# A hybrid attention step on one Trainium2 core: the stores of the attention rows issued by SP among its loads in place of ACT

## What is computed

```
for grp in range(B_GROUPS):
    q, k, v = qkv[:, :, 0, grp], qkv[:, :, 1, grp], qkv[:, :, 2, grp]
    o, lse = _dilated_attn_prompt(q, k, v, B_DILATIONS[grp], P['rel_bias_table'], grp)
    outs.append(o)
    lses.append(lse)
alpha = jax.nn.softmax(jnp.stack(lses, axis=0), axis=0)
attn = jnp.sum(alpha[..., None] * jnp.stack(outs, axis=0).astype(jnp.float32), axis=0)
```

## Time and profile before

| | |
|---|---|
| three runs | 2621.84, 2625.69 and 9907.76 us (one far outlier), median 2625.69 |
| profiled execution | 2629.4 us, span of its instructions 2627.7 us |
| PE busy | 2521.2 us, 96% of the span |
| DVE, ACT, POOL busy | 926.3, 581.7, 511.8 us |
| granted PE clock, mean | 0.981 of full speed |
| DMA, mean | 95 GB/s |

### The profile page before, as it was taken

How to read it: one execution, slowest core, us unless ns; L and a number is a source line. 1 busy time by engine, 2 the same in 40 slices (tenths; PEclk the granted TensorE clock), 3 DMA queues, 4 the chain that set the end, 5 groups by cost and what they waited for, 6 DMA issues and landing times.

```text
span 2627.7 us, 36573 instructions
## 1 busy us (share of the span) xinstructions
PE 2521.2 (96%) x16287; PEld 2398.7 (91%) x16287; DVE 926.3 (35%) x1684; ACT 581.7 (22%) x888; POOL 511.8 (19%) x209
## 2 busy tenths in 40 slices
PE   6999889889999999999999999999999999999998
PEld 5997777568999999999999899988999999999997
DVE  5267653457122222112224512446122222222225
ACT  3212223415211111111112411144211111111112
POOL 2211010102212211212212322122212222112220
PEclk7999999899999999999999999999999999999999
DMA  7522332771212222221221578311111111111101
GB/s 244 192 63 87 98 122 77 244 251 33 81 57 73 97 72 74 81 80 66 81 85 60 171 265 294 126 34 33 49 34 47 49 49 49 47 35 49 49 33 67
DMA packets 163819, 249.10 MB, mean 95 GB/s; under 512 B 6148, under 2 KB 150809, under 8 KB 162382
## 3 DMA queue, kind: packets, MB, share of 16 engines
q1 hardware_dynamic: 150618, 179.29, 20.8%
q0 software_dynamic: 4784, 63.31, 7.0%
q10 hardware_dynamic: 8260, 4.15, 0.6%
HBM read 228.04 MB, written 62.54 MB: 111 GB/s over the span
## 4 chain that ended last, share of the span: by engine, by line
PE 73%; DVE 3%; ACT 2%; DMA 1%; issue 1%; SPq 0%; DVEq 0%
PE ps L2223 66%; PE ps L2323 3%; PE ps L2450 1%; PE ps L2280 1%; DVE h_lo L1489 1%; DVE x L1424 1%; DMA w_raw<-in_e_w_out 0%; PE ps L2346 0%; ACT h_hi L1086 0%; PE ps L2643 0%; ACT nt L1088 0%; DVE nt L1463 0%; PE ps L2458 0%; ACT w_hi L1036 0%; ACT h_hi L1090 0%
## 5 line engine op out<-in xcount | busy, mean ns | idle before, releaser
L2043 POOL TENSOR_TENSOR w_lo<-w_raw,w_hi 128x2048 fp32r<-128x2048 f32 x93 | 432.4, 4649 | 1745.0 <-ACT w_hi L1036 1744.8
L2223 PE MATMUL ps<-h_hi,w_hi 128*128 128x352 f32 x2976 | 656.8, 329 | 6.1 <-ACT tmp L1041 3.0
L2223 PE MATMUL ps<-h_hi,w_lo 128*128 128x352 f32 x2976 | 642.3, 323 | 0.0
L2223 PE MATMUL ps<-h_lo,w_hi 128*128 128x352 f32 x2976 | 641.6, 324 | 0.0
L2223 PEld LDWEIGHTS ps<-h_hi,w_hi 128*128 128x128 f32 x2976 | 502.4, 189 | 26.0 <-issue 23.1
L2223 PEld LDWEIGHTS ps<-h_hi,w_lo 128*128 128x128 f32 x2976 | 511.3, 188 | 0.0
L2223 PEld LDWEIGHTS ps<-h_lo,w_hi 128*128 128x128 f32 x2976 | 506.7, 188 | 0.0
L1516 DVE SCALAR_TENSOR_TENSOR x<-ps,mod,x 128x704 f32<-128x704 f32 (+1 forms) x384 | 270.6, 746 | 285.4 <-PE ps L2223 285.4
L1565 DVE TENSOR_TENSOR tmp<-ps,tmp 128x1056 f32<-128x1056 f32 x44 | 55.3, 1258 | 722.8 <-PE ps L2223 722.8
L1036 ACT ACTIVATE w_hi<-w_raw 128x2048 fp32r<-128x2048 f32 x92 | 175.8, 1911 | 505.4 <-PE ps L2223 389.6
L2223 PE MATMUL ps<-mid_hi,w_hi 128*128 128x352 f32 x1104 | 241.2, 327 | 0.7 <-issue 0.6
(11 more groups left out here) (328 smaller groups left out, 2028.9 us busy)
## 6 DMA issues: line engine op xcount, KB each, us to landing
w_raw<-in_ada_w SPq DMA_DIRECT2D x48, 1024.0 KB, 6.9
w_raw<-in_ffn_w_gate_up SPq DMA_DIRECT2D x44, 1024.0 KB, 5.1
out_kv_sample<-in_cache_b_kv POOLq DMA_DIRECT2D x8, 4088.0 KB, 20.4
w_raw<-in_ffn_w_down SPq DMA_DIRECT2D x22, 1024.0 KB, 4.9
cache<-in_cache_b_kv SPq DMA_DIRECT2D x28, 512.0 KB, 5.9
w_raw<-in_e_w_in SPq DMA_DIRECT2D x11, 1024.0 KB, 5.5
w_raw<-in_o_w_in SPq DMA_DIRECT2D x10, 1024.0 KB, 12.1
out_kv_sample<-in_cache_b_kv POOLq DMA_DIRECT2D x8, 1016.0 KB, 7.6
```

The lines of the kernel that those rows point to most:

```text
L2043: pool.tensor_tensor(w_lo[raw_of[u].slot], w_raw[raw_of[u].slot], w_hi[u % 2].bitcast(F32), ALU.subtract)\
L2223: mm = pe.matmul(big(t)[:, b, 0:BLK], wt, xt[:, k, b * BLK:b * BLK + BLK], start=(k == 0 and n == 0), stop=(k == K - 1 and n == 2))
```

## The change

The `attend_store` branch is taken out of ACT's walk over the plan, and a function `store_rows` with the same waits, the same addresses, the same sizes and the same semaphores is put into SP's walk, at the same item. Nothing else differs. The stores so move from ACT's DMA queue (queue 10 of the page) to SP's (queue 1), and from behind ACT's instructions to behind SP's loads.

```diff
@@ block.sync @@
+            def store_rows(it):
+                g, j = it.g, it.i
+                step, sb, a = 16 * g + j, j // 2, j % 2
+                misc_evacuated(sp, it.pv[j])
+                rows = d_o[g][:, 132 * a:132 * a + 132]
+                src = o_tile(step)
+                if g == 0:
+                    sp.dma_start(rows[P * sb:P * sb + P, :], src).then_inc(o_stored[o_slot(step)], 16)
+                elif g == 1:
+                    sp.dma_start(rows.rearrange("(i r) c -> r i c", r=4)[sb // 2, P * (sb % 2):P * (sb % 2) + P, :],
+                                  src).then_inc(o_stored[o_slot(step)], 16)
+                else:
+                    for r in range(2):
+                        sp.dma_start(rows.rearrange("(i r) c -> r i c", r=16)[2 * sb + r], src[64 * r:64 * r + 64, :])\
+                            .then_inc(o_stored[o_slot(step)], 16)
...
                 elif it.kind == "s_kt" and it.c == 4:
                     load_cache(it.b + 2)
+                elif it.kind == "attend_store":
+                    store_rows(it)
                 elif it.kind == "s_soft":
                     load_cache(NB + 2)
@@ block.scalar @@
-                elif it.kind == "attend_store":
-                    g, j = it.g, it.i
-                    step, sb, a = 16 * g + j, j // 2, j % 2
-                    misc_evacuated(act, it.pv[j])
...
-                    if g == 0:
-                        act.dma_start(rows[P * sb:P * sb + P, :], src).then_inc(o_stored[o_slot(step)], 16)
...
```

More of the change, by code:

```diff
@@ L1305, in _ @@
                         exponents(it.g, 0)
-                elif it.kind == "attend_store":
-                    g, j = it.g, it.i
-                    step, sb, a = 16 * g + j, j // 2, j % 2
-                    misc_evacuated(act, it.pv[j])
-                    rows = d_o[g][:, 132 * a:132 * a + 132]
-                    src = o_tile(step)
-                    if g == 0:
-                        act.dma_start(rows[P * sb:P * sb + P, :], src).then_inc(o_stored[o_slot(step)], 16)
[L1314 to L1320, removed]
                 elif it.kind == "ln_mean":
```

## The result

Over 22 runs of each, the changed kernel took 2635.57 us in the median (2628.29 to 2640.26) and the kernel before 2626.72. The ratio is 1.0028, 95% interval 1.0019 to 1.0038: +7.4 us, between +5.0 and +10.0. That is no difference at a bound of 2%, but it lies beyond its own uncertainty, and the forecast was -0.8. The profiled execution took 2634.30 us, its span is 2632.6.

The account below looks back on a forecast made before the run. PE, busy 96% of the span, was taken as the bound, with time only in its gaps. Terms -2.6 + 0.7 + 1.1 + 0 = -0.8 us gave 2624.9 us, with an 8-in-10 range of 2614 to 2636.

Parts of the forecast that it names:

- the first term: DVE's eight store waits at the row maximum go, and PE gains part of them: -2.6 us, bounds 0 and -9.6.
- Behind 360 us: Part of the -2.6 us: behind DVE's 1.10 us store wait at 360.56, PE gets back 1.06 us.
- Unit 9's load: Groups 0 and 1: issued at 329.5 instead of 321.08, it delays the `ada` load behind it; +0.7 us, +0.3 to +1.1.
- The other loads: Groups 0 and 1: 18 of the 19 loads on SP keep their moment of issue.
- The third key batch: Start of group 2: two store issues on SP stand ahead of it; +1.1 us, bounds +0.3 and +2.1.
- The tail: Second `e_w_out` load behind two store issues, `nat` read later: 0, between -1.4 and +2.1 us.
- late key batches: Rival, group 2: stores in SP's queue push six key batches by 1.1 us each; 2631.5, or 2638 with clock falls; chance 0.18.
- SP becomes the bound: Rival: store waits hold each `ada` load back whole steps; two steps late cost 96 us, giving 2721; chance 0.02.
- the waits at the maximum: Sign: DVE's waits at the maximum for `scratch_o` are gone, under 1 us.
- the key batch: Sign: PE's wait for the third key batch is 4 to 5 us in place of 3.65.
- the `ada` wait: Sign: PE's wait at the `ada` item near 337 has grown to 3 us, with unit 9's load issued about 329.
- the stretch: Sign: the stretch from 190 to 600 us is within 3 us of 410.

Follow-up runs that it names:

- bsplit: Kernel before with the `w_lo` subtractions of units 6 to 15 cut into four pieces, all stores on ACT: 0.9976, -6.3 us.
- splita: Changed kernel with the `w_lo` subtractions of units 6 to 15 cut into four pieces: 0.9972, -7.4 us against the kernel before.
- early: Kernel before, no store on SP; ACT issues a store that stands directly behind an `ada` copy ahead of it: 1.0012, +3.2 us.
- move: Changed kernel with one convolution tap moved two plan items later, behind the scores' copy and `v_tok` of unit 7: 0.9984, -4.2 us against the kernel before.
- split7: Changed kernel with unit 7's `w_lo` subtraction alone cut into four pieces: 0.9991, -2.4 us against the kernel before.
- moreu: The changed kernel with the tap moved, plus six further 64 KB stores on SP ahead of unit 9's load: 0.9999, -0.3 us against the kernel before.
- g1: Kernel before with only group 1's sixteen stores issued by SP, the others on ACT: 0.9997, -0.8 us.
- one: Kernel before with a single store, step 2 of group 0, on SP: 1.0009, +2.4 us.
- last4: Changed kernel with the stores of steps 12 to 15 of group 0 back on ACT: 1.0002, +0.5 us against the kernel before.
- only4: Kernel before with only the stores of steps 12 to 15 of group 0 on SP: 1.0002, +0.5 us.
- g0: Kernel before with only group 0's sixteen stores issued by SP, the others on ACT: 1.0028, +7.4 us.
- morek: The changed kernel with the tap moved, plus six further 64 KB stores on SP ahead of the third key batch: 1.0017, +4.5 us against the kernel before.

## Why the prediction was wrong

**The step that failed** is the first term: "What PE gets of that is less. Behind the 3.21 us wait PE loses 0.64 + 0.90 = 1.54 us to DVE". The maximum did move, to 238.96 where I had said 239.3, and the waits did go, all eight. But I asked only who waits for DVE, not what the earlier maximum sets going: the exponents, the rounding on ACT, and POOL's subtraction, which then fell 2.5 us earlier among DVE's operations. In place of -1.54 the stretch gave +3.8. Nor was much of the 1.54 the store wait's to give: with the subtraction cut, the stretch takes PE 16.52 us with the store wait of DVE still there (bsplit, 2.95 us) and 16.27 without it (splita). The bounds that I set for this term, 0 to -9.6, had no loss in them, and no reason stood there that excluded one. Both rows of the collision were in the trace of before (DVE 3.83 us beside POOL 4.66 us, an operation that otherwise takes 1.27); I had read only DVE's waits, and a stall *inside* an instruction is not listed as one. Removing the wait at its cause by another road (early), moving the tap (move) and cutting the subtraction (split7) show it.

**Behind 360 us** the size was right: -1.04 for the 1.06 expected. It came partly from another place: the wait of 1.06 us fell only to 0.71, and a wait of 0.56 us for the rows' copy ahead of it went.

**Unit 9's load** was right in mechanism, short in size. It was to go out at 329.5 and went out at 334.24, of which PE's lateness by then is the 4.7 us of difference (it came to k = 15 at 324.74 in place of 319.94); the `ada` load followed 2.3 us behind it. PE lost 1.65 us, for +0.7 with an upper bound of +1.1. The `ada` load behind it took 7.8 us from its issue to PE's start, for the 6.2 of before: the two loads side by side cost more than the 0.3 to 1.1 reckoned. In the kernels with the late load the distance from k = 15 to k = 16 was 18.9 to 20.3 us (20.8 with moreu's six stores), in those without 17.7 to 18.0: 1 to 2.5 us. What PE lost between k = 16 and k = 17 can't be put down to it: that distance is 20.58 us in g1, which has no late load, and 18.77 in move, which has one. It goes with the granted clock: 17.0 to 17.9 us where the mean in that stretch was 0.81 to 0.90, and 20.3 to 21.7 where it was 0.69 to 0.75, with the others between.

**The other loads** of groups 0 and 1 kept their places: among PE's waits for `ada` loads only that at k = 16 grew. **The third key batch**: +1.3 for +1.1, in part by luck. The two issues took 2.31 us, near the 2.07 of ACT's row, not the median, and the batch went out 3.2 us later against PE than before; but PE could start 6.5 us behind its issue, for 8.4 before. PE met no new wait at the following key batches, which disposes of that rival. **The tail**: -0.9 for 0, inside its bounds. The rule of the Trainium skill (DMA: Bandwidth & Descriptors, section Queues, rings and completion order) made it -1.4; the wait for `pT` shrank from 2.42 to 2.17 us only, and a new one of 1.60 us for `acc_s` came ahead of it, so the runs don't decide for the rule.

**The rivals.** None held this case. The one that came nearest in time, late key batches at 2631.5 to 2638, gives the measured value by a mechanism that isn't there. "SP becomes the bound" is refuted. The range of 2614 to 2636 did hold the 2635.57, by its width alone: its upper end was meant for late key batches. Of the signs, the waits at the maximum went and the key batch fits, but the `ada` wait grew to 4.0 in place of 3, the stretch grew by 6.1 us in place of at most 3, and the new wait of 4.36 us for `sc` was under no sign at all.

**The sum.** In the trace PE is 1.0 us early at 191 us, ahead of every store, and 5.1 late at the end, so the stretch lost 6.1 us (the two spans, 2632.6 and 2627.7, differ by 4.9). The named parts are 3.8 for the collision, 1.65 for the load, +1.3 at the key batch, and -1.04 and -0.9 elsewhere: +4.8. The rest goes back to no wait that is named here: +0.5 ahead of k = 10, +1.5 from k = 13 to k = 15, +2.45 up to k = 17, -0.7 ahead of the key batch and -3.0 in the 20 us behind it. What stays open is why each part alone (one and early +2.4 and +3.2, last4 +0.5, only4 +0.5) weighs less than half of both together (+7.4 in the changed kernel and in g0). A profile is one execution, and the intervals nearly allow a plain sum: 3.2 + 0.5 with 3 us of uncertainty each. The mean granted clock was 0.979 in g0 and early, 0.980 in the changed kernel, 0.981 to 0.982 in last4 and only4, so it may be what the clock makes of two stalls, though early, with one, has one of the two lowest; no run here separates that. The opposite gap is as open: taking the collision out of the changed kernel gave 9.8 us (split7) and 11.6 (move), where the stretch got 4.8 and 4.6 shorter. The collision and the late load are shown by the traces; how the 7.4 us divide between them is not.

## What to carry to other kernels

A wait that is removed sets other work going earlier: follow it through every engine that it releases, down to the one that shares something with the engine you freed, and give the term a bound on the side of a loss. Look in the trace for single instructions that take several times their usual length, since the list of waits doesn't show them. Where GpSimd and VectorE both work on SBUF, keep GpSimd's instructions short, or keep what TensorE waits for ahead of the VectorE operation that can be blocked. And look for a queue on which neither a copy stands ahead of a store nor a load behind it: here ACT, one place earlier, was the fastest once the subtraction was cut.

## What the runs showed of the hardware

- VectorE's operation with two SBUF inputs stands still for the rest of a GpSimd subtraction that has begun: 32 columns took 4.49 us for 0.25 (changed kernel), and 1.25 (split7) when the subtraction was cut in four. Operations with an input in PSUM, or with one input, ran at full pace beside it. GpSimd waits in turn: 6.49 us in four pieces for 5.02.
- The issue of a store took SyncE very different times: 0.47 us each for six of 64 KB whose rows lie together, 0.32 in the median for the stores of groups 0 and 1, and 2.31 us for two of group 2's, in a stretch (492 to 496) with a DMA share of 0.98.
- Executions of one kernel differed by up to 20 us with the same instructions (morek, 2622.3 to 2642.9), and the time goes with the mean granted clock: from 0.985 to 0.977, +12.6 us in last4.
